# Late modulation panels in the recurrent branch's tail, no border before mixing, and output by channel tiles: one layer of a hybrid decoder

## The reference

```python
def layer_step(x, c, pos, lw, ...):
    sh1, sc1, g1, sh2, sc2, g2 = jnp.split(c @ lw['ada_w'] + lw['ada_b'], 6, axis=-1)
    h = modulate(rms_norm(x, lw['norm_attn']), sh1, sc1)
    parts = split_in(h @ lw['w_in'])
    ...                                   # sparse attention branch: o_nsa
    o_hg, s_hg = hgrn2(parts[8], parts[9], parts[10], parts[11], lb, lw['hg_norm'], hg_state0)
    mix = jax.nn.sigmoid(parts[12]) * (o_nsa @ lw['w_br_nsa']) + jax.nn.sigmoid(parts[13]) * (o_hg @ lw['w_br_hg'])
    x = x + g1[:, None, :] * (mix @ lw['w_out'])
    h2 = modulate(rms_norm(x, lw['norm_ffn']), sh2, sc2)
    f_out, conv_new = conv_ffn(h2, lw['w_up'], lw['conv_w'], lw['conv_b'], lw['w_down'], conv_buf0)
    x = x + g2[:, None, :] * f_out

def conv_ffn(h, w_up, conv_w, conv_b, w_down, buf):
    u, v = jnp.split(h @ w_up, 2, axis=-1)
    u_ext = jnp.concatenate([buf.astype(u.dtype), u], axis=1)
    y = conv_b
    for j in range(CONV_W):
        y = y + conv_w[j] * u_ext[:, j:j + t]
    return (jax.nn.silu(y) * v) @ w_down, u_ext[:, -(CONV_W - 1):]
```

## Time and profile before

| | us |
|---|---|
| median of 3 runs | 2311.18 |
| lowest, highest | 2309.67, 2312.91 |
| the profiled execution | 2305.29 |
| its span | 2303.5 |
| PE busy in it | 2156.0 (94%) |
| DVE, ACT, POOL busy | 1190.4, 660.4, 590.7 |

### The profile page before, as it was taken

How to read it: one execution, slowest core, us unless ns; L and a number is a source line. 1 busy time by engine, 2 the same in 40 slices (tenths; PEclk the granted TensorE clock), 3 DMA queues, 4 the chain that set the end, 5 groups by cost and what they waited for, 6 DMA issues and landing times. The chain is left out here.

```text
span 2303.5 us, 34296 instructions
## 1 busy us (share of the span) xinstructions
PE 2156.0 (94%) x13481; PEld 1967.1 (85%) x13481; DVE 1190.4 (52%) x2152; ACT 660.4 (29%) x1390; POOL 590.7 (26%) x367
## 2 busy tenths in 40 slices
PE   8999997988869999987999999999999999999996
PEld 3798785666656799987999999899999999999996
DVE  5773465888857167763110333565445444445444
ACT  3332464776744034431111212331111101110100
POOL 0112113444631155541000114422221202221200
PEclk9999897999979999988999999999999999999998
DMA  9021452000026312211333443221111111111101
GB/s 363 25 77 34 130 177 88 1 1 1 1 79 229 115 28 57 57 47 48 87 87 83 149 136 86 73 57 56 56 37 54 39 51 41 52 41 48 45 19 76
DMA packets 168405, 168.83 MB, mean 73 GB/s; under 512 B 10178, under 2 KB 147811, under 8 KB 162932
## 3 DMA queue, kind: packets, MB, share of 16 engines
q1 hardware_dynamic: 160278, 118.16, 17.0%
q0 software_dynamic: 7760, 48.55, 6.3%
q10 hardware_dynamic: 224, 0.08, 0.0%
HBM read 153.19 MB, written 17.87 MB: 74 GB/s over the span
## 5 line engine op out<-in xcount | busy, mean ns | idle before, releaser
L245 PE MATMUL psall<-hT_short,ring_short 128*128 128x344 f32 x1896 | 613.1, 323 | 6.9 <-PEq L1843 5.7
L247 PE MATMUL psall<-hT_short,ring_short 128*128 128x344 f32 x1896 | 606.5, 320 | 0.0
L240 POOL TENSOR_TENSOR ring_short<-ring,ring_short 128x1024 fp32r<-128x1024 f32 (+3 forms) x53 | 201.4, 3802 | 1089.6 <-DVE ring_short L235 768.6
L246 PE MATMUL psall<-work_short,ring_short 128*128 128x344 f32 x1392 | 446.4, 321 | 0.0
L245 PEld LDWEIGHTS psall<-hT_short,ring_short 128*128 128x128 f32 x1896 | 357.5, 189 | 7.9 <-issue 6.8
L247 PEld LDWEIGHTS psall<-hT_short,ring_short 128*128 128x128 f32 x1896 | 357.4, 189 | 0.0
L246 PEld LDWEIGHTS psall<-work_short,ring_short 128*128 128x128 f32 x1392 | 263.0, 189 | 0.2
L3060 DVE SCALAR_TENSOR_TENSOR xT<-psall,mod,xT 128x344 f32<-128x344 f32 (+1 forms) x264 | 151.4, 573 | 129.7 <-PE psall L247 126.6
L246 PE MATMUL psall<-xT_short,ring_short 128*128 128x344 f32 x648 | 207.5, 320 | 0.0
L245 PE MATMUL psall<-work_short,work_short 128*128 128x344 f32 x528 | 176.3, 334 | 2.9 <-POOL work_short L240 2.9
L2971 ACT ACTIVATE work<-psall 128x344 f32<-128x344 f32 (+1 forms) x66 | 30.0, 456 | 503.9 <-PE psall L247 503.0
(11 more groups left out here) (445 smaller groups left out, 4031.7 us busy)
## 6 DMA issues: line engine op xcount, KB each, us to landing
ring<-in_w_up SPq DMA_DIRECT2D x44, 512.0 KB, 5.0
ring<-in_w_in SPq DMA_DIRECT2D x27, 512.0 KB, 5.1
work<-in_ada_w SPq DMA_DIRECT2D x23, 512.0 KB, 4.1
work<-in_w_down SPq DMA_DIRECT2D x10, 1024.0 KB, 4.9
ring<-in_ada_w SPq DMA_DIRECT2D x9, 512.0 KB, 4.4
x_spill<-xT SPq DMA_DIRECT2D x4, 1032.0 KB, 14.8
xT<-x_spill SPq DMA_DIRECT2D x4, 1032.0 KB, 7.4
ring<-in_ada_w SPq DMA_DIRECT2D x4, 1024.0 KB, 17.5
```

Of the source, the lines that this page charges most:

```text
L240: return eng.tensor_tensor(lo, src, hi, ALU.subtract)
L245: pe.matmul(out, w[0], x[0], start=first, stop=False)
L246: pe.matmul(out, w[0], x[1], start=False, stop=False)
L247: return pe.matmul(out, w[1], x[0], start=False, stop=last)
```

## The change

It has three parts. (1) The recurrence is no longer a block: its programs (`hgrn_programs`) run ahead of mixing in the FFN's block. Sixteen of the late panels are made in slots 36 to 42, two per slot, and two behind them, from four homes in `work` that are free by then, into bank 1; DVE reads them before it scales the last output. The last `turn_output` stands behind the first half-round of gate products. The first gate weights are cut at slot 38 (DVE) and lowered at slot 40 (POOL). The other sixteen panels stay as they were. (2) In group 10's body DVE handles the last hidden tile between the additions of tiles 2 to 4. (3) The last down products are followed, tile by tile, by transposes of the conv rows and of the finished channel tile; ACT copies, SP stores 128 columns of all 1024 rows (pieces of 512 bytes) from four buffers. The output block is gone.

The diff, without changes of indentation and cut to its core:

```diff
+    def sync(sp):
...
+        sp.wait_ge(level, OUTS * (HGH - 1))
+        sp.wait_ge(dec_out, HGH - 1)
+        panels.load(sp, 0)
+        sp.wait_ge(diff, 8 * (HGH - 1))
+        panels.load(sp, 1)
         sp.wait_ge(projected, SLOTS * HGH)
         next_weights.load(sp, 0)
+        sp.wait_ge(gated, HGH)
+        panels.load(sp, 2)
+        sp.wait_ge(o_read, HGH - 1)
+        panels.load(sp, 3)
+        for p in range(4, panels.TAIL):
+            sp.wait_ge(panels.used, p - 3)
+            panels.load(sp, p)
+        sp.wait_ge(o_ready, HGH)
+        sp.wait_ge(states_out, 32 * HGH)
...
             if u == 1 and h:
                 turn_output(h - 1)
+            if n >= SLOTS * HGH:
+                wait(pe, evac, SLOTS * HGH)
+                panels.sum(pe, 2 * (n - SLOTS * HGH))
             if u >= 0:
                 attend(h, u)
-            turn_output(HGH - 1)
+            if n >= SLOTS * HGH:
+                panels.sum(pe, 2 * (n - SLOTS * HGH) + 1)
+        for p in range(2 * (LAST - SLOTS * HGH), panels.TAIL):
+            panels.sum(pe, p)
...
-            scale_output(HGH - 1)
-            next_weights.take_high(v, 0)
+            if n == LAST - 5:
+                next_weights.take_high(v, 0)
+        panels.finish(v, 0)
+        scale_output(HGH - 1)
         finish(HGH - 1)
-            v.wait_ge(o_read, HGH)
...
+        self.tail = [view(s.work, at, KT, P) for at in (8256, 10320, 9288, 11352)]
...
+    def sum(self, pe, q):
+        src, i, times = self.home(q)
+        at = 9 * (q % self.TAIL)
+        pe.wait_ge(self.loaded[i], 16 * times)
+        for k in range(KT):
+            last = pe.matmul(self.banks[q // self.TAIL][:, at:at + 9], src[:, k, :], self.s.cT[:, k, :],
+                             start=(k == 0), stop=(k == KT - 1))
+        last.then_inc(self.used, 1)
...
+                    if n == 0:
+                        if (b, c) == (0, 1):
+                            pe.wait_ge(panels.read, 1)
+                        elif (b, c) == (0, 2):
+                            pe.wait_ge(hgrn.picked, hgrn.PICKS)
+                        elif (b, c) == (1, 2):
+                            pe.wait_ge(hgrn.rstd_d_ready, HGH)
...
-                modulate(2 * n + b)
-        modulate(EARLY)
-        modulate(EARLY + 1)
+                if (n, b) == (0, 0):
+                    turn_output(HGH - 1)
+        pe.wait_ge(hgrn.o_read, HGH)
+        panels.sum(pe, TAIL)
+        panels.sum(pe, TAIL + 1)
...
+            if n == 1:
+                act.wait_ge(hgrn.o_read, HGH)
+                act.wait_ge(hgrn.dec_done, HGH)
...
+                            if not more and n == 2:
+                                hide(2 * g + 1, 1, par, c)
+                            elif not more and (n, c) == (3, 1):
+                                hidden_high(1, par)
+                            elif not more and (n, c) == (4, 1):
+                                hidden_low(1, par)
-                if up:
+                if up and more:
                     hidden(2 * g + 1, 1, par)
...
+            def turn_output(n):
+                pe.wait_ge(added, finished(n))
+                wait(pe, y_copied, 2 * (n - 1))
+                for t in range(TT):
+                    last = pe.transpose(y_banks(n)[:, t, :], x[:, n, t * P:(t + 1) * P], s.ident[:, :])
...
+                if n < TURNS:
+                    turn_tails(n)
+                if n:
+                    turn_output(n - 1)
+            turn_output(KT - 1)
...
+                sp.dma_start(y_prompt[:, tiles, n * P:(n + 1) * P], y_out[n % 4][:, tiles, :]).then_inc(sent[n % 4], 16)
```

More of the change, by code:

```diff
@@ new lines, in hgrn_programs, with __init__, home, load @@
+    hgrn = Core()
+    hgrn.sync, hgrn.gpsimd, hgrn.scalar, hgrn.tensor, hgrn.vector = sync, gpsimd, scalar, tensor, vector
+    hgrn.o_turned, hgrn.o_read, hgrn.dec_done = o_turned, o_read, dec_done
+    hgrn.rstd_d_ready, hgrn.picked, hgrn.PICKS = rstd_d_ready, picked, OUTS * HGH
+    return hgrn
+class LatePanels:
+    TAIL, COUNT, FIRST = 2 * KT, 4 * KT, G1
+    def __init__(self, s, T):
+        self.s = s
+        self.ada = T["ada_w"].rearrange("(k p) n -> p k n", p=P)
+        self.tail = [view(s.work, at, KT, P) for at in (8256, 10320, 9288, 11352)]
+        self.border = [view(s.ring, 2048 + 1024 * i, KT, P) for i in range(2)]
+        self.late = [view(s.work, 24768, KT, P), view(s.ring, 7168, KT, P)]
+        self.loaded = [s.sem(f"l_loaded{i}") for i in range(8)]
+        self.used, self.read = s.sem("l_used"), s.sem("l_read")
+        self.banks = s.ps[1], s.ps[6]
+    def home(self, q):
+        if q < self.TAIL:
+            return self.tail[q % 4], q % 4, q // 4 + 1
+        i = q - self.TAIL
+        return (self.border[i], 4 + i, 1) if i < 2 else (self.late[i % 2], 6 + i % 2, i // 2)
+    def load(self, sp, q):
+        dst, i, _ = self.home(q)
+        c = (self.FIRST + q) * P
+        sp.dma_start(dst, self.ada[:, :, c:c + P]).then_inc(self.loaded[i], 16)
+    def sum(self, pe, q):
[6 more added lines that the diff above has]
+        last.then_inc(self.used, 1)
+    def finish(self, v, part):
+        v.wait_ge(self.used, self.TAIL * (part + 1))
+        first = self.FIRST + self.TAIL * part
+        finish_modulation(self.s, v, first, first + self.TAIL, self.banks[part])
+        v.nop().then_inc(self.read, 1)
@@ L2516, in sync @@
                 outs.load(sp, 0)
-        sp.wait_ge(panel_used, PANELS)
+        sp.wait_ge(panels.used, PANELS)
         outs.load(sp, 1)
@@ L2544, in tensor @@
     def tensor(pe):
[L2545 to L2550 removed]
+        turn_output = hgrn.tensor(pe)
         for n in range(KT):
@@ L2987, in _, with copy_tails, copy_output @@
             groups(act, body, 8, ch)
+            def copy_tails(q):
+                act.wait_ge(turned, q + 1)
+                cols = slice(512 * q, min(512 * q + 512, DFF))
+                act.activation(rows[0:NB + 2, cols], s.ps[5][0:NB + 2, 0:cols.stop - cols.start], ACT.Copy).then_inc(copied, 1)
+            def copy_output(n, half):
+                act.wait_ge(y_turned, 2 * n + half + 1)
+                tiles = slice(HALF * half, HALF * half + HALF)
+                act.activation(y_out[n % 4][:, tiles, :], y_banks(n)[:, tiles, :], ACT.Copy).then_inc(y_copied, 1)
+            for n in range(KT):
+                if n < TURNS:
+                    copy_tails(n)
+                if n:
+                    wait(act, sent[(n - 1) % 4], 16 * ((n - 1) // 4))
+                    for half in range(2):
+                        copy_output(n - 1, half)
+            act.wait_ge(sent[3], 16)
+            copy_output(KT - 1, 0)
+            act.wait_ge(dec_turned, 1)
+            act.activation(y_dec[:, 0:512], s.ps[4][0:NB, :], ACT.Copy).then_inc(dec_copied, 1)
         @block.vector
```

1003 lines of the change are left out of this document (491 added, 512 removed).

## The result

| | us |
|---|---|
| median before, beside it | 2311.95 (2309.67 to 2312.91) |
| median after | 2285.6 (2285.19 to 2285.93) |
| ratio | 0.9891, 95% interval 0.9874 to 0.9907 |
| profiled execution, its span | 2285.93, 2282.9 |
| forecast, its range | 2268.0, 2261 to 2282 |

The account below looks back on a forecast made before the run. TensorE, busy in 94% of the span, was taken to pace most of the kernel. −27.2 + 3.6 − 19.6 = −43.2 us gave 2262.1 for the profiled execution; 5.9 put on the median gave 2268.0, range 2261 to 2282.

Parts of the forecast that it names:

- part 1: Gate stage: sixteen panels leave the gate products, where TensorE bounds, at 1.70 us each; 27.2 us gained.
- part 2: Recurrence's tail: the sixteen panels go there and the border vanishes; gates start at 1073, 3.6 us lost.
- part 3: Kernel's end: hidden tile interleaved with additions, output transposed and stored by channel tile behind down products; 19.6 us gained.
- The blocked VectorE instruction: Tail, beside GpSimd's low part of gate weights: blocked 0 to 4.5 us, less 1.7 cover; 2 us taken, including half-clock panels.
- The interleaved steps of the hidden tile: Last hidden tile's multiply, cast and subtraction among additions: bursts on VectorE cost 1.7 us, while the 4.29 us wait goes.
- The forecast's lower bound, 21.5: Kernel's end: if the interleaving costs nothing, 21.5 us gained instead of 19.6.
- (a): Rival, tail gets long: slow panel loads, five panels at half clock, VectorE blocked; 11.5 us more, 2279.5; chance 0.15.
- (b): Rival, first gate round: the border's wait returns as TensorE waits for normalised output; up to 7.6 us, 2275.6; chance 0.07.
- (c): Rival, end: stores in 512-byte pieces pace it; 48 us worst case, 2284 at 6 us a store; chance 0.05.
- (d): Rival, tail: panels loaded one by one, 10.3 us each; gates at 1152, 2347 us, slower than before; chance 0.03.
- (e): Rival, tail: no room left, so 32 panels still cost TensorE-bound time; 27.2 us returns, 2295; chance 0.04.
- the signs named: Right: gates near 1073 at full clock, no idle border. Wrong: panel-load waits, late key transposes, blocked level 5, slow stores.

Follow-up runs that it names:

- e6: e3 with panel 6 multiplied 13 times in a row, instead of once, between gate products far from the tail; 2328.93 us in one run.
- e4: The changed kernel with twelve unused products of 344 columns behind each of the sixteen tail panels; 2286.8 us in one run.
- e8: The changed kernel with operands of its sixteen tail panels exchanged (nine vectors as weights, panel moving), their results unused; 2261.26 us.
- e9: The changed kernel with operands of its sixteen tail panels exchanged and their results copied, transposed and used, nothing left out; 2266.64 us.
- e10: e6 with the operands exchanged in only the twelve extra multiplications of panel 6, results unused; 2309.84 us in one run.
- e2: The changed kernel with the FFN and output blocks of before, so only panels in the tail and no border; 2308.04 us, ratio 0.9995.
- e3: The changed kernel with no panel in the tail: all 32 between gate and branch products, no border, new end; 2286.06 us.
- e5: e3 with both parts of the first gate weights made by VectorE in slot 42, GpSimd's low part gone; 2279.24 us.
- e1: The kernel before with only the changed FFN (hidden tile among additions, output by channel tiles) and no output block; 2287.7 us.
- e7: e5 with the weight split in slot 37 and the first two gate tiles made behind slots 37 and 39; 2271.84 us.

## Why the prediction was wrong, step by step

| | forecast | in the two profiles |
|---|---|---|
| gate stage (part 1) | −27.2 | −27.6 |
| level at 1019 to the gates (part 2) | about +4 | +24.5 |
| end (part 3) | −19.6 | −21.3 |

The three add up to −24.4 us; with the 4.1 us by which the profile of after runs late ahead of the tail they give −20.3, against −20.6 between the two spans. The medians differ by 26.4. The table also rests on these rows of before:

```profile
1019.00 3.67 PE L1972 MATMUL psall<-ring 128*128 128x64 f32 x16 [3.35 <-DVE ring L2210]
...
1280.44 3.81 PE L2549 MATMUL psall<-cT,ring 128*128 128x9 f32 x32
...
2220.11 0.58 DVE L3060 SCALAR_TENSOR_TENSOR xT<-psall,mod,xT 128x344 f32<-128x344 f32 x1 [6.58 <-PE psall L247]
```

**Part 1 was right.** From the first gate product to the border's panels were 211.37 us, from 1069.07 to 1280.44, and now 183.76, from 1097.62 to 1281.38. Sixteen panels at their 1.70 us make 27.2 of it. The product behind a panel is 0.24 us ahead of the next one instead of 0.16, which makes 1.3 more, and the last transposes, which now stand here, take back 0.9.

**Part 2 failed, in one sentence: "with panels 0 and 1 filling the earlier gap I expect the clock to be mostly up".** From the level-2 products to the gates the forecast had 1073 − 1019 = 54 us; measured were 1097.62 − 1023.09 = 74.5, against 50.1 before. On that sentence rest the two terms that were mis-sized: the recurrence's products at 15.0 us and the panels at 1.70 each (11 of them, 18.7). I had read the 0.50 of the earlier trace rows as the price of the gaps, and expected filled gaps to cure it. The runs showed something else: the clock went down while TensorE computed nine-column products with a weight load each, without a gap (e6), and it was down for most of the tail that holds sixteen such panels (after); the same panels with wide products beside them (e4) or with 128 columns moving (e8, e9, e10) left it mostly up. At half clock a panel cost 3.4 us, and the levels, updates, diagonals and decode products between the panels paid too.

Held against e9, start to start, the 20.4 us come out whole. The 15 panels of this stretch take 40.3 us in the changed kernel (six at 3.4, three at 2.9, six at 1.7 to 2.0) and 28.5 in e9. All other products take 34.3 and 21.4. Waiting takes nothing and 4.3. So about half of the lost time is the panels' own and half their neighbours'. It ate most of what part 1 gave, which e2 shows directly: −1.3 us for both together, which is not clear of no change.

The rest of part 2's walk came out close wherever the clock was up. In e9 the way from that level to the gates is 1080.85 − 1026.70 = 54.15 us, against the 54 forecast, and the whole kernel gained 43.6 us, against 43.2. That agreement is partly luck: an exchanged panel takes 1.80 to 1.83 us, the end gave 1.7 more than forecast, one burst of updates in e9 still went at half clock (3.59 us), and nothing waited for the blocked weighing. Panel 2 landed, put on before's time by the level (1026.70 − 1019.00 = 7.7), at 1025.65; forecast was 1026.1. The key transposes in the changed kernel start 10.26 us behind the level, where 8.8 were forecast: the level and two panels fill those 10.26 us at half clock, without a gap.

The Trainium skill, TensorE: Matmul & The Clock Gate, section Why this matters for your kernels, gives idle gaps between bursts as what lowers the clock. The trace differs here: in e6 it fell with no gap. Gaps may well do their part (e8 has 0.74 in the window behind its wait of 2.84 us). But e9 has two waits behind that level, 4.3 us in all, and its tail came out at the length forecast, while the changed kernel's has none and is 20 us longer. The level itself shows it most closely: it stands behind panel 0 and a gap in both, 1.62 us in the changed kernel, where it takes 3.67 us, and 1.51 in e9, where it takes 2.00. The measurement decides: in this tail, what TensorE computed mattered more than whether it computed.

**The blocked VectorE instruction** came as bounded: 4.99 us where the bound was 4.5. The 2 us that I set for it cost nothing in the changed kernel: I had counted only panel 6 as cover, but the updates (3.5 us, at half clock) and panel 5 stand ahead of level 5 as well; e3 pays it (4.13 us of waiting), and e5 gets it back (5.5 us more gained than e3). The 4.99 row beside GpSimd's 4.51, which began 0.07 us earlier, agrees with what the Trainium skill, SBUF — State Buffer, section Who interferes with whom, says of the shared port.

**Part 3 was right**, 1.7 us too cautious. From the first addition of the last group to the span's end it is 21.3 us shorter (2220.84 to 2282.9, before 2220.11 to 2303.5), and e1 alone gives −21.6. The interleaved steps of the hidden tile cost 0.8 instead of the 1.7 us charged: from that first addition to the first of the last down products are 23.78 us (2220.84 to 2244.62), before 27.30 with the wait of 4.29 in it. (The forecast's lower bound, 21.5, is 0.2 more than its own 19.6 + 1.7.)

**Rivals.** (a) had the right mechanism and the wrong size: it priced five panels at half clock, 8 us, where the 15 panels cost 14.8 us more than at 1.70 each and the recurrence's products, which it left out, went slow as well. "The gaps get filled", its counterargument, was the error itself. Its 2279.5 lies 6.1 us under the measured 2285.6. (b) did not occur: TensorE has no wait between 1023 and 1300. (c) did not: stores landed in 3.2 to 4.0 us, so its 2284, for stores of 6 us, is near only by chance. (d) did not: the panels were never waited for. (e) gave 27.2 back for a reason that was not there, the lack of room; by luck, that sum is near the tail's own 24.5 us. Of the signs named, the VectorE instruction of over 4 us came, but level 5 did not wait for it; the gates' first product, expected near 1073 and at full clock, came at 1097.62 at half clock (0.53 to 1101).

What stays open: which property of a product decides, its columns, or the weight load that each few columns need. Exchanging the operands changes both at once, and no run here separates them. Nor is it shown why the clock came back for a while inside the changed kernel's tail (two panels in 4.06 us at 1052, in 3.64 at 1085), although the same products went on. Levels 2 and 3 stay at half clock in e7, where no panel stands beside them; they stand behind waits of 3.35 and 1.92 us and ahead of the first gate tile, and no run tells whether the waits are the reason.

## What to carry to other kernels

Don't price work that moves into a half-clock stretch at the full-clock row. Filling the gaps didn't by itself bring the clock up here: ask whether what fills them keeps it up, and price the neighbours too. Where many products with few columns per weight load stand in a row, try turning them round, so that the small operand is the weights and the large one moves; here that was 21.1 instead of 40.3 us for the same 96 products, nearly all of it by the clock. Before two changes are believed to add up, time each alone: here the one with the intricate plan gave 1 us and the plain one 21.

## What was not expected of the hardware

- TensorE's granted clock fell from 1.00 to 0.50 while it was busy for 10.00 of every 10 us, in products of 9 columns; in products of 128 columns, at the same place, it stayed at 1.00 (e6 and e10, one execution each).
- 192 unused products of 344 columns put into the changed kernel's tail cost 1.2 us, one run against a median, or 3.8 when each is held against before beside it.
- Products that load a 128x9 block as weights and move 128 columns took 1.8 us for 8, against 1.70 for 8 that load 128x128 and move 9 at full clock: nearly the same price, without the fall of the clock.
- Stores of 512 KB in pieces of 512 bytes landed in a median of 3.2 us, where those in rows of 4 KB took 2.7; TensorE never waited for them, as all but the last had a channel tile of products to land behind.
